# Two transformer blocks on one core: TensorE waits for its own last product at three places, one weight load and one silu move

## The reference

```
# first block
u = rms_norm(x) @ w_in                  # lru_x, lru_g, q, k, v
x = x + [norm(gelu(lru_g) * lru(conv(lru_x))), norm(stick_breaking(q, k, v))] @ w_out
gu = rms_norm(x) @ w_ffn_in
x = x + (silu(gu[:2816]) * gu[2816:]) @ w_ffn_out
x = rms_norm(x)
# second block
cb, cc, cin, q, k, v, f, g = split(rms_norm(x) @ w_in_2)
u = dwconv(cc * cin);  y_conv = (cb * u) @ w_out_conv;  y_attn = forgetting_attention(q, k, v, f) @ w_out_attn
x = x + (sigmoid(g0) * y_conv + sigmoid(g1) * y_attn) @ w_o
up = dwconv(rms_norm(x) @ w_up);  a, b = split(up)
x = x + (silu(a) * b) @ w_down
return rms_norm(x)
```

## Time and profile before

| | us |
|---|---|
| median of 3 runs (lowest, highest) | 1262.15 (1261.77, 1264.3) |
| the profiled execution's own time | 1258.74 |
| its span, first to last instruction | 1257.0 |
| TensorE busy | 1228.9 |
| VectorE busy | 993.6 |
| ScalarE busy | 667.6 |

### The profile page before, as it was taken

How to read it: one execution, slowest core, us unless ns; L and a number is a source line. 1 busy time by engine, 2 the same in 40 slices (tenths; PEclk the granted TensorE clock), 3 DMA queues, 4 the chain that set the end, 5 groups by cost and what they waited for, 6 DMA issues and landing times.

```text
span 1257.0 us, 19170 instructions
## 1 busy us (share of the span) xinstructions
PE 1228.9 (98%) x7805; PEld 1078.8 (86%) x7805; DVE 993.6 (79%) x1200; ACT 667.6 (53%) x833; POOL 186.3 (15%) x168
## 2 busy tenths in 40 slices
PE   6999999999999999999999999999999999999997
PEld 5878677889999999997899999657888999988886
DVE  6788764878778688987989857566588889979886
ACT  6462674374455346567544535462344666656555
POOL 5003010002222111200222113000000223202020
PEclk9999999999999999999999999999999999999999
DMA  5423201259999779564599958200424799958765
GB/s 172 142 68 101 68 1 34 84 136 185 183 206 181 133 217 259 126 112 128 111 210 199 188 89 218 101 1 34 134 68 151 141 210 188 183 145 176 208 114 138
DMA packets 144458, 174.14 MB, mean 139 GB/s; under 512 B 5370, under 2 KB 118250, under 8 KB 144242
## 3 DMA queue, kind: packets, MB, share of 16 engines
q0 software_dynamic: 58288, 71.33, 35.3%
q1 hardware_dynamic: 86066, 101.58, 24.4%
q10 hardware_dynamic: 16, 0.00, 0.0%
HBM read 170.78 MB, written 2.11 MB: 138 GB/s over the span
## 4 chain that ended last, share of the span: by engine, by line
PE 95%; ACT 2%; DVE 2%; issue 1%; DMA 1%; SPq 0%; ACTq 0%
PE psum L2492 12%; PE psum L2494 12%; PE psum L2493 12%; PE psum L2758 11%; PE psum L2757 11%; PE psum L2759 11%; PE psum L3035 3%; PE psum L3034 3%; PE psum L3033 3%; PE psum L2829 3%; PE psum L2830 3%; PE psum L2831 3%; PE psum L2942 1%; PE psum L2632 1%; PE psum L2617 1%; PE psum L2644 1%
## 5 line engine op out<-in xcount | busy, mean ns | idle before, releaser
L988 ACT ACTIVATE w_hi<-raw 128x1024 fp32r<-128x1024 f32 (+2 forms) x121 | 156.3, 1293 | 210.3 <-PE psum L2494 147.8
L1536 DVE TENSOR_TENSOR w_lo<-raw,w_hi 128x1024 fp32r<-128x1024 f32 (+2 forms) x121 | 184.6, 1527 | 58.6 <-ACT w_hi L988 58.6
L2492 PE MATMUL psum<-act_hi,w_hi 128*128 128x512 f32 x520 | 207.9, 400 | 4.4 <-DVE act_lo L1545 1.7
L2494 PE MATMUL psum<-act_hi,w_lo 128*128 128x512 f32 x520 | 204.4, 393 | 0.0
L2493 PE MATMUL psum<-act_lo,w_hi 128*128 128x512 f32 x520 | 203.6, 392 | 0.0
L2757 PE MATMUL psum<-s_hi,w_hi 128*128 128x256 f32 x704 | 195.2, 277 | 1.4 <-issue 1.4
L2758 PE MATMUL psum<-s_lo,w_hi 128*128 128x256 f32 x704 | 195.2, 277 | 0.0
L2759 PE MATMUL psum<-s_hi,w_lo 128*128 128x256 f32 x704 | 195.0, 277 | 0.0
L2757 PE MATMUL psum<-act_hi,w_hi 128*128 128x256 f32 x528 | 146.4, 277 | 0.4 <-ACT scratch L1355 0.4
L2758 PE MATMUL psum<-act_lo,w_hi 128*128 128x256 f32 x528 | 146.5, 277 | 0.0
L2759 PE MATMUL psum<-act_hi,w_lo 128*128 128x256 f32 x528 | 146.3, 277 | 0.0
(11 more groups left out here) (413 smaller groups left out, 2690.5 us busy)
## 6 DMA issues: line engine op xcount, KB each, us to landing
raw<-in_w_in SPq DMA_DIRECT2D x15, 1024.0 KB, 5.3
xz<-in_w_ffn_in POOLq DMA_DIRECT2D x24, 512.0 KB, 6.6
raw<-in_w_ffn_in SPq DMA_DIRECT2D x22, 512.0 KB, 5.4
xz<-in_w_up POOLq DMA_DIRECT2D x21, 512.0 KB, 6.0
raw<-in_w_up SPq DMA_DIRECT2D x18, 512.0 KB, 5.2
raw<-in_w_in SPq DMA_DIRECT2D x16, 512.0 KB, 4.9
v<-in_w_in POOLq DMA_DIRECT2D x15, 512.0 KB, 6.3
x_buf<-in_w_ffn_out POOLq DMA_DIRECT2D x6, 1024.0 KB, 10.4
```

The costliest lines, as they stand in the source:

```text
L988: A(w_at(w_hi, s, h, n - h), home(s, n)[:, h:n], ACT.Copy).then_inc(w_hi_ready, 1)
L1536: V.tensor_tensor(w_at(w_lo, s, h, n - h), home(s, n)[:, h:n], w_at(w_hi, s, h, n - h).bitcast(F32), ALU.subtract).then_inc(w_lo_ready, 1)
L2492: mm(dst, stationary[0], moving[0], start=first, stop=False)
L2494: return mm(dst, stationary[1], moving[0], start=False, stop=last)
```

## The change

Three things. TensorE waits at three places until its own last product is finished: ahead of the full-size slab ("gate", 1) of the first block's feed-forward, ahead of the two full-size slabs q0 and q1 (for the one-column products of turn_row), and ahead of the last full-size slab of the second feed-forward. Each of these slabs is the last full-size work ahead of a row of half-size products. The transfer of ("out", 1) leaves its place behind ("p2", 5) and goes behind ("p4", 5), where MIXES is 7. gate_silu(i - 2) is issued at ("p0", i), behind the copy of that product and the weight splits that follow it, instead of gate_silu(i - 1) at ("p4", i).

```diff
                     if (kind, i) == ("p2", MIXES - 2):
-                        load_slab(mix_at("out", 1))
                         sp.wait_ge(w_lo_ready, mix_at("p2", MIXES - 3) + 1)
                         load_slab(mix_at("out", 0))
+                    if (kind, i) == ("p4", MIXES - 2):
+                        load_slab(mix_at("out", 1))
...
+                if kind == "p0" and i > SECOND_SEVEN + 1 or kind == "gate0":
+                    gate_silu(i - 2)
                 if kind == "p1" and i > SECOND_SEVEN:
                     gate_taps(i - 1)
                 if kind == "p4" and i > SECOND_SEVEN:
                     up_taps(i - 1)
-                    gate_silu(i - 1)
...
                 if kind == "gate":
+                    pe.wait_ge(slab_done, up_at(kind, i))
                     slab_a(up_at(kind, i), bank=6)
...
             turn_row(rstd[:, RSTD_AT[N_MIX2]], bank_of(GROUP[S_K2]) + 3)
+            pe.wait_ge(row_turned, 2)
             wait_banks(GROUP[S_Q2B])
...
                 wait_banks(GROUP[s])
+                if s == S_UP + 2 * SECOND_SEVEN - 1:
+                    pe.wait_ge(slab_done, s)
                 slab_a(s, half=half_done if s == S_UP + 2 * SECOND_SEVEN - 1 else None)
```

## The result

The changed kernel is slower: 1272.44 us median (1271.35 to 1273.26, 4 runs) against 1262.53 for the kernel before (1261.77 to 1264.3, 4 runs), ratio 1.0076, 95% interval 1.0059 to 1.0093. I had predicted 1256.2 in a range up to 1262. The profiled execution took 1273.26 us, 14.5 us more than that of before (1258.74).

The account below looks back on a forecast made before the run. TensorE was taken as the bound, busy 1228.9 of 1257.0 us. First row +0.2, second -3.7, third -2.5, together -6.0 us: 1252.7 against the profile's 1258.74, 1256.2 against the median; range 1250.5 to 1262.

Parts of the forecast that it names:

- the waits fix the lot, and as fast, since fast is the commoner: All three half-size rows: TensorE restarted by its own product always takes the fast pace, up to 5.9 us gained.
- -5.9 us for the three rows: Slow products turned fast at 4.5 ns each: first row -0.1, second -3.6, third -2.2 us.
- its own sign of being wrong: 117.8 ns a product in the first row or in the down product behind it would show the prediction wrong.
- the first wait turns the first row slow: Rival: first row and down product turn slow, 2172 products, +9.8 us, end at 1266 us; chance 0.12.
- The waits' own cost: At the three waits: 0.34 us each, 0.25 behind the transposed row, together +0.9 us.
- The load's move: Second row: moving ("out", 1) removes the 1.56 us stop at ("p1", 4), -1.6 us.
- The silu's move: Third row: the copy ends 1.0 us earlier, removing TensorE's stop ahead of 1016.23, -0.6 us.
- the brief wait at 1059.75: Third row: a weight load waiting briefly for VectorE, slow pace behind it; taken as gone through the silu's move.
- A faster second row: Second row: 792 slow products turned fast, -3.6 us, less 1.2 us for new waits.
- VectorE or the transfers are the bound: Rival, second row: stop stays or moves and the faster pace is waited away; total -2.5, 1259.7 us; chance 0.17.
- new waits: Second row: faster TensorE runs into VectorE, 95% busy; put at +1.2 us, between 0 and 3.1.
- The 3.4 us between profile and median: Profiled 1258.74 against median 1262.15 us: perhaps 750 slow products that the profiled execution happened not to have.

Follow-up runs that it names:

- Run 10: Kernel before with ScalarE's copy of (p1, 2) waiting for ffn_hidden 3 instead of 4, plus the load's move, no waits: 1260.77 us, ratio 0.9968.
- run 9: Kernel before with only ScalarE's copy of (p1, 2) waiting for ffn_hidden 3 instead of 4: 1262.91 us, ratio 0.9992.
- run 1: Changed kernel without its three waits, so both moves alone: 1259.35 us, ratio 0.9955 to the kernel before.
- run 7: Changed kernel without its third wait: 1266.71 us, one execution.
- run 12: Kernel before with both moves and the copy of (p1, 2) waiting for ffn_hidden 3 instead of 4, no waits: 1255.62 us, ratio 0.9933.
- run 8: Kernel before with both moves and the first wait, without the extra product ahead of ("p0", 2): 1259.55 us, ratio 0.994.
- run 11: Kernel before with the silu's move and the copy of (p1, 2) waiting for ffn_hidden 3 instead of 4, no waits: 1260.43 us, ratio 0.9962.
- run 2: Kernel before with only the first wait added, ahead of ("gate", 1): 1272.61 us, ratio 1.0037.
- Run 3: Kernel before with only the second wait added, for row_turned ahead of q0: 1264.11 us, ratio 0.9994.
- run 5: Changed kernel without the extra product ahead of ("p0", 2), whose result nothing reads: 1262.0 us, ratio 0.9963 to the kernel before.

## Why the prediction was wrong, step by step

**The step that failed** is "I take it that the waits fix the lot, and as fast, since fast is the commoner". The first half held: a wait for the own last product does not draw, it turns the pattern by a step that was the same each time for the first wait (a to c, 5 of 5) and for the third (c to a, 4 of 4); for the second it varied (a to c, a to a, c to a, b to c in the five traces with it). Without that wait the same place turned a to a, b to a and c to c, in nine traces of nine; so this wait made the start of the second row less regular, not more. The second half was a guess from how often a pace had been seen, about a thing that isn't drawn. The third wait turns a row from fast to slow. The first turns its slab to c, which would be the good one, but the extra product of 229 ns behind it starts ("p0", 2) slow and leaves the next slabs, and with them the first row and the down product, at a. In place of -5.9 us for the three rows stands +14.8 in the profiled pair. "Fast is the commoner" was thin, too: the rows that the prediction names there were fast in four of seven cases, not in two of three. And its own sign of being wrong came true, 117.8 ns in the first row and in the down product.

**The rival that came true** is the third, with a chance of 0.12: the first wait turns the first row slow. Its price, 9.8 us, measured 5.55 + 4.4. It was put at 1266 only because it kept my gains in the other rows; the third row and the pieces of the second were slow as well.

**The waits' own cost**, 0.9 us, was right: 0.34, 0.22 and 0.35. By the Trainium skill ("TensorE: Matmul & The Clock Gate", Single matmul latency) I had estimated 0.17 us a wait; the rows of this case, twice that, decide. The same page of the Trainium skill (A second HAM failure mode: psum-queue depth-cycling) speaks of frequent short idle times, and I had called the trace in disagreement with it because of one stop of 1.56 us. That was too much: one stop tests nothing of the kind. The granted clock is 1.00 in every window above, and no run here shows more.

**The load's move**, -1.6 us, was about right in size and wrong in kind. The stop didn't go: in the changed kernel 0.40 and 1.25 us stand where 1.56 stood. But over the traces the second row takes 94.1 us on average with the move (92.5 to 95.1, 8 traces) and 96.3 without (94.9 to 98.9, 6 traces). Run 10 against run 9, which differ in this move alone, gives the same: 94.01 and 96.32 us. So the move is worth some 2 us, seen over many traces; the pair before and after shows none, and the times of runs 9 and 10 scatter too much to confirm it.

**The silu's move**, -0.6 us, can be right for the stop at ("p0", 5), and the brief wait at 1059.75 goes with it. I had counted the pace behind that wait to the waits' account. In runs 1, 7 and 12, which lack the third wait, the third row is fast to its end: 125.12 against 127.58, that is 2.4 us, of which 1.8 is pace that a stop of 35 ns had cost. But in runs 8 and 11, which have the move and no third wait either, a stop stands in the row all the same, and it took 129.53 and 129.03 us. The five average 126.8; the five traces with neither the move nor the third wait (before, 2, 3, 9, 10: 126.25 to 129.48) average 127.8. So the move makes a clean row possible and does not ensure it: 1 us on average, from few traces.

**A faster second row**: the rival *VectorE or the transfers are the bound* (0.17) was right there in the main. Run 3 gave the row its fast start and it ended no sooner; in the changed kernel VectorE has no gap ahead of the late z_m0. With the load moved a part came through: runs 7 and 12, which started fast, took 93.53 and 92.53 us, the six that started slow 93.84 to 95.06, 94.5 on average. That is 1.4 us where I had put 3.6 less 1.2 for new waits.

**The 3.4 us between profile and median** I had read as some 750 products that are slow in the other executions. What they are stays open, for the executions behind that median, 1261.77 to 1264.3 us, are all short ones. The large spread is another matter: of 31 executions of before, 14 took over 1268 us and most others 1258 to 1265, about 10 us apart, which is what the first row and the down product differ by, 2244 products at 4.45 ns. The first wait puts all of them into the slow group, and that would be why the changed kernel scatters so little. That the long executions of before are those with a slow first row is argued from this size and from the profiles of runs 8, 9 and 10, not seen in each.

**Open.** What in the engine makes the spacings of 226, 229 and 232 ns, and why a half-size product behind the long one keeps 113.3 ns and another 117.8. Why some stops of tens or hundreds of ns turn the pace and others don't. Why the second wait turned the pattern in several ways.

## What to carry to other kernels

When the same instructions run at two paces under the same granted clock, look for an order that they inherit from what ran ahead before taking it for chance; a synchronisation that makes such an order repeatable can make the bad one repeatable, so test one wait at a time, and in both directions. In a kernel near its TensorE bound look for waits of tens of ns inside the long rows, for here two of them cost far less than the slow pace of the hundreds of products behind them. A faster pace buys little in a row that another engine bounds. And where the executions of one kernel spread over 15 us, as here, three or four of them say little about a change of a few us.

## What the runs showed of the hardware

- Half-size products (256 columns) run at 113.3 or 117.8 ns, both at a granted clock of 1.00; full-size ones at 229 ns on average, as 226, 229, 232 in turn.
- The pace of half-size products follows the last full-size spacing ahead: 231 ns or more, fast, 79 of 79; 230 or less, slow, 77 of 77; behind a single product in between, slow, 12 of 12.
- A wait of TensorE for its own last product costs 0.34 to 0.35 us; the first one turned the pattern from a to c in 5 traces of 5, the third from c to a in 4 of 4.
- A stop of 25 ns (run 8) or 35 ns (before, 1059.8) changed the pace for 1199 and 407 products in a row; stops of 93 ns (run 1), 147 and 513 ns (run 5) didn't.
